# Conv FFN gate and up products: 512-column matmuls of high and low input parts, and a GpSimd add

## The reference, cut to what matters

```
def conv_ffn(h, w_up, w_dw, b_dw, w_down):        # h: 256 tokens x 1024
    a, v = jnp.split(h @ w_up, 2, axis=-1)         # 2 x 2816 columns
    return (jax.nn.silu(causal_dwconv(a, w_dw, b_dw)) * v) @ w_down

x = x + conv_ffn(rmsnorm_2(x, ffn_norm_g[i]), ffn_w_up[i], ...)
```

## Time and profile before

| | us |
|---|---|
| time before, median of 3 runs (1827.78 to 1830.97) | 1828.81 |
| span of the profiled execution, first to last instruction | 1824.4 |
| TensorE busy | 1775.6 |
| VectorE busy | 1324.4 |
| ScalarE busy | 989.7 |
| GpSimd busy | 435.7 |
| first conv FFN, its gate and up products begin at | 1256.4 |
| second conv FFN, the same | 1629.4 |

### The profile page before, as it was taken

One profiled execution on the slowest core, in us unless ns is written; L12 is line 12 of the kernel. 1 busy time (PEld: TensorE's weight loads), 2 busy tenths in 40 slices (PEclk: granted clock), 3 DMA queues, 4 the chain that ended last, 5 costly groups with the idle time before them and its releaser, 6 DMA issues.

```text
span 1824.4 us, 36159 instructions
## 1 busy us (share of the span) xinstructions
PE 1775.6 (97%) x14392; PEld 1710.4 (94%) x14394; DVE 1324.4 (73%) x1817; ACT 989.7 (54%) x1470; POOL 435.7 (24%) x444
## 2 busy tenths in 40 slices
PE   5999999999999999999999999999999999999998
PEld 4999999969999999999889999979999989589998
DVE  6787879889777577778966555887666757866665
ACT  4554566574554565546565445676445533864443
POOL 1232200061222132220233211473222100532221
PEclk9999999999999999999999999999999999999999
DMA  9877745718667657776725555414555533035551
GB/s 399 351 276 293 297 155 184 276 71 323 226 253 276 253 194 276 277 276 229 297 93 184 184 184 184 142 67 142 184 185 184 180 141 138 24 116 185 184 184 70
DMA packets 51351, 371.14 MB, mean 203 GB/s; under 512 B 5696, under 2 KB 5952, under 8 KB 6336
## 3 DMA queue, kind: packets, MB, share of 16 engines
q1 hardware_dynamic: 42048, 302.85, 45.5%
q0 software_dynamic: 9216, 67.11, 9.5%
HBM read 368.89 MB, written 1.05 MB: 203 GB/s over the span
## 4 chain that ended last, share of the span: by engine, by line
PE 84%; DVE 6%; ACT 3%; issue 3%; DMA 1%; POOL 1%; SPq 0%; POOLq 0%; DVEq 0%; ACTq 0%
PE gu L756 40%; PE acc L763 8%; PE acc L764 8%; PE acc L765 8%; PE gu L1308 2%; PE gu L763 2%; PE gu L765 2%; PE gu L764 2%; PE gu L1143 2%; DVE w_lo L2041 1%; DMA mring<-in_mods 1%; DVE mring L2056 1%; PE acc L1379 1%; PE acc L1280 1%; ACT w_hi L1529 1%
## 5 line engine op out<-in xcount | busy, mean ns | idle before, releaser
L2041 DVE TENSOR_TENSOR w_lo<-ring,w_hi 128x2048 fp32r<-128x2048 f32 x244 | 564.2, 2316 | 242.2 <-ACT w_hi L1529 242.0
L1529 ACT ACTIVATE w_hi<-ring 128x2048 fp32r<-128x2048 f32 x244 | 464.8, 1907 | 59.1 <-PE acc L765 43.4
L756 PE MATMUL gu<-Hs_hi,w_hi 128*128 128x258 f32 (+1 forms) x2080 | 419.7, 283 | 0.4 <-ACT arena L1563 0.4
L756 PE MATMUL gu<-Hs_lo,w_hi 128*128 128x258 f32 (+1 forms) x2080 | 416.6, 282 | 0.0
L756 PE MATMUL gu<-Hs_hi,w_lo 128*128 128x258 f32 (+1 forms) x2080 | 416.1, 281 | 0.0
L697 POOL TENSOR_TENSOR arena<-arena,rstd 128x512 f32<-128x512 f32 x132 | 209.0, 1583 | 813.0 <-ACT arena L1563 775.8
L756 PEld LDWEIGHTS gu<-Hs_hi,w_hi 128*128 128x128 f32 x2080 | 320.4, 189 | 0.9 <-ACT arena L1563 0.6
L756 PEld LDWEIGHTS gu<-Hs_hi,w_lo 128*128 128x128 f32 x2080 | 320.4, 189 | 0.0
L756 PEld LDWEIGHTS gu<-Hs_lo,w_hi 128*128 128x128 f32 x2080 | 320.0, 189 | 0.0
L764 PE MATMUL acc<-hid_lo,w_hi 128*128 128x256 f32 x1056 | 298.0, 282 | 0.0
L763 PE MATMUL acc<-hid_hi,w_hi 128*128 128x256 f32 x1056 | 296.6, 281 | 0.8 <-DVE hid_lo L2228 0.8
(11 more groups left out here) (420 smaller groups left out, 3094.2 us busy)
## 6 DMA issues: line engine op xcount, KB each, us to landing
ring<-in_weights SPq DMA_DIRECT2D x276, 1024.0 KB, 4.8
mring<-in_mods POOLq DMA_DIRECT2D x64, 1024.0 KB, 5.7
mring<-in_mods SPq DMA_DIRECT2D x8, 1024.0 KB, 8.4
con<-in_constants SPq DMA_DIRECT2D x1, 1344.0 KB, 15.3
X<-in_x SPq DMA_DIRECT2D x1, 1024.0 KB, 11.3
out<-X SPq DMA_DIRECT2D x1, 1024.0 KB, 3.9
cact<-in_c SPq DMA_DIRECT2D x1, 512.0 KB, 3.4
small<-in_small SPq DMA_DIRECT2D x1, 448.0 KB, 23.0
```

Source lines behind the costliest of these rows:

```text
L756: ins = mm(dst, part, x_lo if i == 1 else x_hi, start=start and i == 0, stop=stop and i == 2, skip_group_check=True)
L1529: act.activation(w_hi[buffer_of(n0, s)][:, :], ring[:, n % RING, :], ACT.Copy).then_inc(hi_ready, 1)
L2041: dve.tensor_tensor(w_lo[b][:, :], ring[:, n % RING, :], w_hi[b][:, :].bitcast(F32), ALU.subtract).then_inc(split_ready, 1)
```

## The change

In the two conv FFNs, `gate_up` issues for each feature tile and each of gate and up one matmul of 512 columns, w_hi against x_hi and x_lo side by side (an access pattern with two runs of 256, one in `Hs_hi` and one in `Hs_lo`), so that w_hi x_hi falls in the first half of the bank and w_hi x_lo in the second. w_lo x_hi is added to the first half by a matmul of 256 columns. ScalarE's copy takes the whole of both banks, 1024 values in each partition, into a larger buffer `cw`. GpSimd first adds the second half to the first, waits until that is written, and then multiplies by `row` as before. The other FFNs stay as they are.

```diff
+        HALVES = (arena_at - h_at) // 4 + ARENA
+        halves = nc.alloc_sbuf_tensor_at("halves", [P, HALVES], F32R, offset=h_at)
+
+        def half_at(at, *shape):
+            return halves[:, at:at + int(np.prod(shape))].rearrange("p (a b) -> p a b", a=shape[0])
+
+        def two_parts(hi, lo):
+            return bass.AP(hi.tensor, hi.offset, [[HALVES, P], [lo.offset - hi.offset, 2], [1, hi.shape[-1]]])
...
+        cw = part(10 * L + 160, 2, 2, 2 * L)
-        Hs_hi = rounded("Hs_hi", 32 * L, KD, LS)
-        Hs_lo = nc.alloc_sbuf_tensor_at("Hs_lo", [P, KD, LS], F32R, offset=h_at)
+        Hs_hi = half_at((arena_at - h_at) // 4 + 32 * L, KD, LS)
+        Hs_lo = half_at(0, KD, LS)
...
 GpSimd, ffn(name):
                     pool.wait_ge(pair_free, FREE_AT[name] + f + 1)
                     both = cp[:, f % 2, :, 0:L]
+                    if name[0] == "c":
+                        both = cw[:, f % 2, :, 0:L]
+                        pool.tensor_tensor(both, both, cw[:, f % 2, :, L:2 * L], ALU.add).then_inc(halves_added, 1)
+                        pool.wait_ge(halves_added, NF * (name == "cffn1") + f + 1)
                     pool.tensor_tensor(both, both, row.unsqueeze(1).to_broadcast([P, 2, L]), ALU.mult).then_inc(scaled_ready, 1)
...
 TensorE:
+            def wide(banks, w, cols, x_hi, x_lo, start, stop):
+                for n, bank in enumerate(banks):
+                    mm(bank, w_hi[w][:, cols[n]], two_parts(x_hi, x_lo), start=start, stop=False, skip_group_check=True)
+                for n, bank in enumerate(banks):
+                    ins = mm(bank[:, 0:L], w_lo[w][:, cols[n]], x_hi, start=False, stop=stop, skip_group_check=True)
+                return ins
...
+                        if width == L:
+                            ins = wide([gu[:, 2 * (f % 2) + e, :] for e in range(2)], buffer_of(n0, s),
+                                       [slice(k * L + e * P, k * L + (e + 1) * P) for e in range(2)],
+                                       Hs_hi[:, k, 0:L], Hs_lo[:, k, 0:L], start=(k == 0), stop=(k == KD - 1))
+                            continue
...
 ScalarE, ffn(n0, conv):
-                width = L if conv else LS
+                width = 2 * L if conv else LS
...
-                        a, c = act_buf[:, f % 2, :], cp[:, f % 2, :, :]
+                        a, c = act_buf[:, f % 2, :], (cw if conv else cp)[:, f % 2, :, :]
...
 VectorE, ffn(n0, i):
-                        o, a, b = act_buf[:, f % 2, :], cp[:, f % 2, 0, 0:L], cp[:, f % 2, 1, 0:L]
+                        c = cp if i is None else cw
+                        o, a, b = act_buf[:, f % 2, :], c[:, f % 2, 0, 0:L], c[:, f % 2, 1, 0:L]
```

More of the change, by code:

```diff
@@ L434, in build @@
         scaled_ready = sem("scaled_ready")
+        halves_added = sem("halves_added")
         mul_ready = sem("mul_ready")
```

## The result

The changed kernel takes 1905.21 us (median of 4 runs, 1902.33 to 1907.00); the kernel before, on the same chip, 1828.37 (4 runs, 1827.78 to 1830.97). The ratio is 1.0416, with a 95% interval of 1.0401 to 1.0431: slower. Forecast were 1898 and a range of 1872 to 1925. The profiled span grew by 79.5 us, from 1824.4 to 1903.9, which is more than the 76.8 of the medians. The reason lies in the profile of before: in every run listed for this case the time lies 1.7 to 1.9 us above the span of the same execution (here 1905.68 against 1903.9), so that profile shows an execution of about 1826.2 us (an estimate), quicker than each of the four timed ones.

What follows compares the result with a forecast made beforehand. TensorE's 17.06 us round was taken as the bound, with a 16.67 us loop close behind. Per conv FFN 21.0 + 12.1 + 1.47 = 34.5 us; twice, 69 on 1824.4 gives 1893.4, plus 4.4 outside the span: 1898 us, range 1872 to 1925.

Steps and rivals of the forecast that it cites:

- The bound before, and the loop behind it: Conv FFN rounds before the change: TensorE bounds at 17.06 us; a loop over ScalarE, GpSimd and VectorE takes 16.67.
- TensorE's saving: `gate_up` products in the conv FFNs: 35 ns saved a feature tile, 0.56 us a round, TensorE's round then 16.50 us.
- the first rival: Conv FFNs: the extra work is hidden and TensorE's saving shows, 12 us saved, 1816 us; chance 4%.
- The bad end: TensorE's 512-column fp32r matmul at 347 ns, from the 384-column row, making the round 20.6 us; not taken.
- Copy: ScalarE's copy from the banks: 512 more values cost 0.41 us, so it takes 1.00 us.
- Add and multiplication: GpSimd in each conv tile: add 1.20 us, gap 0.14, then multiplication; with the copy an odd tile costs 1.75 more.
- The even tile, half hidden: Even tile after a `down` slot: longer copy and add hide beside VectorE's `low`, leaving 0.14 + 1.20 = 1.34 us.
- Tile 0: First tile of a conv FFN: norm row 0.28 us earlier, copy +0.41, add and multiplication +1.34, together 1.47 us.
- TensorE stalls, and does not push back: Conv FFN rounds: TensorE stalls 3.3 us a round without delaying the 19.76 us loop, so its saving is worth nothing.
- the sign that was named: Profile after: TensorE idle ahead of products, released by `low`, 3 us a round.
- Nothing else: Outside the conv FFNs' loop: other stages and other FFNs keep their code and stay unchanged; weight DMAs only get more time.
- The rival of a falling clock: TensorE's clock falls to 0.81 in the stalls, round 20.4 us, 13 us more, 1911 us; chance 3%.

Runs made afterwards that it cites:

- e1: Changed kernel without GpSimd's add of the second half and the wait behind it; wide products and wide copy stay: 1843.98 us, ratio 1.0082.
- e6: Kernel before the change, with ScalarE's and VectorE's work reordered so the odd tile's copy precedes the even tile's SiLU and `hid_hi`: 1829.80 us, ratio 1.0001.
- e2: Changed kernel without GpSimd's add and its wait, and with the copy as wide as before, leaving the wide products and `cw`: 1832.68 us, ratio 1.0019.
- e4: Changed kernel with the rows of `cw` 514 values apart instead of 512, nothing left out: 1902.77 us, ratio 1.0403.
- e3: Changed kernel with the six 256-column matmuls of the kernel before; wide copy and GpSimd's add stay: 1906.62 us, ratio 1.0423.

## Why the prediction was right, step by step

- **The bound before, and the loop behind it.** Right. The loop of 16.67 us a round behind TensorE's 17.06 left 0.39 us. e1 shows that 0.6 us a round use this up (0.41 of the copy in the odd tile and 0.1 of the multiplication in each), and e6 that a shorter loop is worth nothing below TensorE's round.
- **TensorE's saving.** This term was mis-sized: the products save 10 ns a feature tile (712.5 to 702) and not 35. The row taken was of bf16 matmuls, 220 ns; in fp32r 512 columns take 233. It cost the forecast nothing, since the saving was counted at nothing, but the first rival, with at most 3.7 us saved, would have reached 1825 at best and not 1816; e2 measured 1833. The bad end, 347 ns, did not come.
- **Copy.** Right: it takes 1.00 us, as forecast.
- **Add and multiplication.** The mechanism was right and the sizes were short. The forecast was 1.20 for both and a gap of 0.14; measured were 1.30 for the add, 1.29 for the multiplication and a gap of 1726.28 - 1724.90 - 1.30 = 0.08. So +0.10, +0.09 and -0.06 make 0.13, and the odd tile cost 10.31 - 8.41 = 1.90 in place of 1.75. e4 shows that the multiplication's part comes from the rows being 512 apart.
- **The even tile, half hidden.** Right in kind: the add took the blocked place beside `low`, 2.49 us, and the multiplication followed in full. The tile cost 9.73 - 8.26 = 1.47 in place of 1.34, again 0.13 more.
- **Tile 0.** It cost 1.9 us more, in place of 1.47: 0.13 are the sizes again, and 0.2 come from a `gate_up` that is shorter by 8 x 10 ns = 0.08 us and not by 0.28.
- **TensorE stalls, and does not push back.** Right in kind: TensorE stands idle up to 2.7 us at a time, until `low` ends, and e3, with the old products, runs at the same pace. But the sign that was named, 3 us of idle time a round, did not come: it was 1.8, and the other 1.25 us went into slower matmuls at a mean clock of 0.95.
- **Nothing else.** Not quite. The last `down` was left at its old price; the standstill ahead of it grew from 0.4 to 7.15 us in the second conv FFN, and it ran at a granted clock of 0.67, 2.4 us more. The rival of a falling clock was placed in the rounds. There the clock did fall, to a mean of 0.95, and cost nothing, since the loop, with no copy waiting for products, set the pace; it was this last stretch that paid.

In sum, the forecast span of 1893.4 was low by 10.5 us: 2 x (37.1 - 34.5) = 5.2 from the sizes, 2.4 from the clock, 0.4 and 2.6 of other shifts. The 4.4 us that the prediction added for what lies outside the span were no fixed amount: 1.8 of them are, and 2.6 came from a profile of an execution quicker than the median. The median after lies only 1905.2 - 1903.9 = 1.3 above the profiled span, so 3.1 of the 10.5 came back, and the forecast of 1898 was low by 7.3. These 3.1 and the 2.6 us of shift ahead of the conv FFNs nearly cancel. That is luck in the sum, and small beside the 74 us that the conv FFNs cost.

## What to carry to other kernels

When work is moved off the busiest engine, look for a loop of waits over the others and take its round from the timeline, not from busy shares: here engines at 54% and 24% were part of a loop 2.3% short of the bound, and 3.3 us a round more in it cost 77 us while the saving was worth at most 3.7. The same addition cost 9 us in all where it read the second operand from the banks, on the faster engine, ahead of the work that blocks its neighbour. And before a product is made wider for speed, measure the wide one in the same type.

## What the runs showed of the hardware that was not expected

- fp32r matmuls with moving data of 256 columns start 118 to 119 ns apart, of 512 columns 233 (from two runs far apart) or 236 (one run read twice), bf16 ones of 512 220: a wide fp32r matmul saves 2% against two of 256.
- GpSimd's multiplication of 512 values takes 1.29 us where the two rows of its operand are 512 values apart, 1.19 to 1.20 at 258 and 514. Its add takes 1.30 at 512 and at 514.
- VectorE's `tensor_scalar` on 256 values took 1.20 us in place of 0.41 beside GpSimd's add, which kept its 1.28.
- Around a standstill of 7.15 us TensorE's granted clock went to its lower level (0.50, 1.2 GHz) and stayed there for the first 24 matmuls behind it, 5.3 us; they started 0.213 us apart in place of 0.118. With products of zeros in the gap it was 1.00. Idle time of 2.63 us in a round was followed by 0.50 as well.
- Open: the copy of tile 0 of the first conv FFN, behind code that is the same in all these kernels, came 2.1 to 5.9 us later in their profiles than in that of before. Some 2 us are to be expected, since that one shows a quick execution. By the starts of `high`, the delay of the changed kernel's profile arises in pieces: 1.7 us between 350 and 416 us, 0.5 given back between 796 and 836, 1.5 between 1145 and 1215. No run isolates it, and it limits what single profiles say of a few us.
